# Expert scatter of a two-layer flow-matching step on one core: single passes over a high and a low part, and two units of the next job ahead of it

## The reference, cut to what matters

```
for e in range(N_EXPERTS):
    out = out + combine[:, e:e + 1] * swiglu(xt, exp_wg[e], exp_wu[e], exp_wd[e])
```

## Time and profile before

| | |
|---|---|
| median of 3 runs | 1936.82 us (1935.96 to 1938.35) |
| profiled execution, its own time | 1934.04 us |
| its span, first to last instruction | 1932.3 us |
| mean granted TensorE clock | 0.954 |
| PE, DVE, ACT busy | 91%, 66%, 51% |

### The profile page before, as it was taken

One profiled execution on the slowest core, in us unless ns is written; L12 is line 12 of the kernel. 1 busy time (PEld: TensorE's weight loads), 2 busy tenths in 40 slices (PEclk: granted clock), 3 DMA queues, 4 the chain that ended last, 5 costly groups with the idle time before them and its releaser, 6 DMA issues.

```text
span 1932.3 us, 32651 instructions
## 1 busy us (share of the span) xinstructions
PE 1767.5 (91%) x11466; PEld 1430.8 (74%) x11466; DVE 1284.7 (66%) x1889; ACT 985.6 (51%) x1356; POOL 132.3 (7%) x208
## 2 busy tenths in 40 slices
PE   4989999977979998898669999999999999999997
PEld 2757777756768884797558788887878787878785
DVE  4345666665255551322379898989888898989897
ACT  1322222221234443122248787877777777878684
POOL 0134333330000000110000000000000000000000
PEclk8889999988989998899869999999999999999999
DMA  9531111020755437433339898988989797979790
GB/s 402 211 142 41 41 41 41 3 90 17 316 228 183 152 135 290 152 135 135 155 119 370 302 366 315 369 333 344 351 326 370 295 372 298 379 303 367 307 351 22
DMA packets 61367, 442.86 MB, mean 229 GB/s; under 512 B 7008, under 2 KB 8160, under 8 KB 10080
## 3 DMA queue, kind: packets, MB, share of 16 engines
q1 hardware_dynamic: 59184, 437.81, 59.3%
q10 hardware_dynamic: 1584, 2.79, 0.4%
q0 software_dynamic: 512, 1.05, 0.2%
HBM read 438.99 MB, written 2.62 MB: 229 GB/s over the span
## 4 chain that ended last, share of the span: by engine, by line
PE 81%; DVE 8%; issue 4%; DMA 3%; ACT 2%; POOL 1%; DVEq 0%; ACTq 0%; POOLq 0%; SPq 0%
PE PS L865 33%; PE PS L894 17%; PE PS L616 4%; PE PS L953 3%; PE PS L593 3%; PE PS L1044 2%; PE PS L699 2%; PE PS L1067 2%; PE PS L573 2%; PE PS L557 2%; DMA MIX<-w_mod 2%; PE PS L958 1%; PE PS L882 1%; DVE LO L1501 1%; PE PS L679 1%
## 5 line engine op out<-in xcount | busy, mean ns | idle before, releaser
L1501 DVE TENSOR_TENSOR LO<-W,HI 128x1024 fp32r<-128x1024 f32 x662 | 781.9, 1222 | 111.7 <-ACT HI L1101 65.2
L1101 ACT ACTIVATE HI<-W 128x1024 fp32r<-128x1024 f32 x662 | 689.7, 1062 | 137.4 <-PE PS L865 77.5
L865 PE MATMUL PS<-HI,XHI 128*128 128x512 f32 x970 | 393.5, 406 | 16.4 <-ACT XHI L1300 14.1
L865 PE MATMUL PS<-HI,XLO 128*128 128x512 f32 x970 | 380.6, 392 | 0.0
L865 PE MATMUL PS<-LO,XHI 128*128 128x512 f32 x970 | 294.8, 393 | 9.1 <-DVE LO L1501 8.5
L865 PEld LDWEIGHTS PS<-HI,XHI 128*128 128x128 f32 x970 | 183.1, 189 | 55.6 <-issue 15.8
L865 PEld LDWEIGHTS PS<-LO,XHI 128*128 128x128 f32 x970 | 181.3, 188 | 55.6 <-DVE LO L1501 16.3
L865 PEld LDWEIGHTS PS<-HI,XLO 128*128 128x128 f32 x970 | 183.5, 189 | 34.9
L894 PE MATMUL PS<-HI,HHI 128*128 128x512 f32 x484 | 188.9, 390 | 1.5 <-ACT HHI L1277 1.5
L894 PE MATMUL PS<-HI,HLO 128*128 128x512 f32 x484 | 188.3, 389 | 0.0
L894 PE MATMUL PS<-LO,HHI 128*128 128x512 f32 x484 | 145.5, 389 | 0.0
(11 more groups left out here) (285 smaller groups left out, 2160.0 us busy)
## 6 DMA issues: line engine op xcount, KB each, us to landing
W<-w_exp SPq DMA_DIRECT2D x298, 1024.0 KB, 6.9
W<-w_ffn SPq DMA_DIRECT2D x33, 1024.0 KB, 4.9
W<-w_mod SPq DMA_DIRECT2D x32, 1024.0 KB, 13.0
MIX<-w_mod SPq DMA_DIRECT2D x16, 1024.0 KB, 16.8
W<-w_rkv SPq DMA_DIRECT2D x8, 1792.0 KB, 8.2
W<-w_qkv SPq DMA_DIRECT2D x8, 1536.0 KB, 7.9
W<-w_o SPq DMA_DIRECT2D x1, 4096.0 KB, 12.0
W<-w_o SPq DMA_DIRECT2D x1, 3072.0 KB, 11.1
```

The costliest lines, as they stand in the source:

```text
L865: last = mm(PS[2 * (s % 2) + g], x[:, 2 * n + k, T * g:T * g + T], w[:, 512 * k:512 * k + 512], start=(n == 0 and k == 0 and i == 0 and le ...
L1101: fn(HI[:, u % NBUF], raw_unit(phase, u), ACT.Copy).then_inc(hi_ready, 1)
L1501: tt(LO[:, u % NBUF], raw_unit(phase, u), HI[:, u % NBUF].bitcast(F32), ALU.subtract)\
```

## The change

On PE the scatter's two-pass float32 products become two single-pass float32r products each, of a high part YHI and a low part YLO of the output with SELT, the turned selection of ones and zeros. The weight of each slot is applied before that: turn_weights turns SELR instead of SELW, and gets the slot's weight as a column, the product of SELW with a column of ones (two products, one for each group of tokens); DVE copies the column to SLOTW. ACT's copy of the output multiplies with SLOTW and writes YHI; DVE then computes bank * SLOTW - YHI into YLO, one operation for each half, before its additions, and PE waits for these (`ey_low`). YHI and YLO lie in the unused half of XHI and XLO. first_unit now does units 0 and 1 of the next job ahead of the scatter, and swiglu starts at unit 2.

```diff
+        SELT = sb("SELT", TT, F32R)
...
-        SELWT = flat[1][:, D + 2 * TT:D + 3 * TT]
...
+        SLOTW = sb("SLOTW", 1)
+        YHI, YLO = XHI[:, :, SLOTS:2 * SLOTS], XLO[:, :, SLOTS:2 * SLOTS]
...
                     for n in range(4):
-                        if phase == "ffn" or s or n:
+                        if phase == "ffn" or s or n > 1:
                             gate_up(phase, base, j, s, n, groups)
...
             def turn_weights(j):
                 pe.wait_ge(sel_ready, j + 1)
                 for g in range(G):
-                    last = nc.tensor.transpose(PS[2][:, P * g:P * g + P], SELW[:, g], IDENT)
+                    nc.tensor.transpose(PS[2][:, P * g:P * g + P], SELR[:, g].bitcast(F32), IDENT)
+                for g in range(G):
+                    last = mm(PS[2][:, TT:TT + 1], SELW[:, g], ONES[:, 0:1], start=(g == 0), stop=(g == G - 1))
                 last.then_inc(selT_psum, 1)
 
             def first_unit(j):
                 pe.wait_ge(xhi_ready, j + 1)
                 pe.wait_ge(x_split, j + 1)
-                gate_up("exp", NS * j + NS, j, 0, 0, 1)
+                for n in range(2):
+                    gate_up("exp", NS * j + NS, j, 0, n, 1)
 
             def job(j):
                 swiglu("exp", NS * j + NS, j, 1, lambda: gather(j + 1))
                 turn_weights(j + 1)
                 first_unit(j + 1)
-                pe.wait_ge(ey_sbuf, j + 1)
                 for b in range(4):
+                    if b % 2 == 0:
+                        pe.wait_ge(ey_low, 2 * j + b // 2 + 1)
                     for half in range(2):
                         c = 2 * b + half
-                        last = mm(PS[(6, 7, 1, 3)[b]][:, TT * half:TT * half + TT], YNAT[:, 0, P * c:P * c + P],
-                                  SELWT, start=True, stop=True)
+                        out = PS[(6, 7, 1, 3)[b]][:, TT * half:TT * half + TT]
+                        mm(out, YHI[:, c], SELT, start=True, stop=False)
+                        last = mm(out, YLO[:, c], SELT, start=False, stop=True)
                     last.then_inc(scat_psum, 1)
...
                 for half in range(2):
-                    last = fn(YNAT[:, 0, 512 * half:512 * half + 512], PS[4 + half], ACT.Copy)
-                last.then_inc(ey_sbuf, 1)
+                    fn(YHI[:, 4 * half:4 * half + 4], PS[4 + half].rearrange("p (c d) -> p c d", c=4), ACT.Copy,
+                       scale=SLOTW).then_inc(ey_sbuf, 1)
...
                 dve.wait_ge(selT_psum, j + 1)
-                nc.vector.tensor_copy(SELWT, PS[2][:, 0:TT]).then_inc(selT_sbuf, 1)
+                nc.vector.tensor_copy(SELT, PS[2][:, 0:TT])
+                nc.vector.tensor_copy(SLOTW, PS[2][:, TT:TT + 1]).then_inc(selT_sbuf, 1)
...
                 split("exp", 2 * FFN_LOADS + 1, j)
+                for half in range(2):
+                    dve.wait_ge(ey_sbuf, 2 * j + half + 1)
+                    stt(YLO[:, 4 * half:4 * half + 4], PS[4 + half].rearrange("p (c d) -> p c d", c=4), SLOTW,
+                        YHI[:, 4 * half:4 * half + 4].bitcast(F32), ALU.mult, ALU.subtract).then_inc(ey_low, 1)
                 for b in range(4):
```

More of the change, by code:

```diff
@@ L162, in build @@
         SELR = sb("SELR", TT, F32R).rearrange("p (g s) -> p g s", g=G)
-        sb("B1HIGH", C * TT - D - TT)
+        sb("B1MID", TT)
+        SELT = sb("SELT", TT, F32R)
+        sb("B1HIGH", C * TT - D - 3 * TT)
         HT, B = HTB[:, 0], [HTB[:, 1], HTB[:, 2], sb("B2", C * TT).rearrange("p (c t) -> p c t", c=C)]
@@ L347, in build @@
         selT_psum, selT_sbuf = sem("selT_psum"), sem("selT_sbuf")
-        ey_psum, ey_sbuf, scat_psum, scat_acc = sem("ey_psum"), sem("ey_sbuf"), sem("scat_psum"), sem("scat_acc")
+        ey_psum, ey_low, ey_sbuf, scat_psum, scat_acc = sem("ey_psum"), sem("ey_low"), sem("ey_sbuf"), sem("scat_psum"), sem("scat_acc")
         y_out, moe_done = sem("y_out"), sem("moe_done")
```

## The result

The changed kernel takes 1949.9 us (median of six runs, 1944.9 to 1956.8), the kernel before 1936.4 beside it: a ratio of 1.0074, 95% interval 1.0049 to 1.0098, so about 14 us slower. The forecast was 1943.2, in a range of 1937.5 to 1956.0. Direction and range held; the size was twice the forecast's +6.4.

A forecast was written before the change was run, and what follows sets the result against it. The boundary between jobs was taken as bound by the DVE chain from the scatter's additions, not PE's work; 0.62 + 0.09 = 0.71 us later at nine boundaries gives +6.4 us, 1943.2 against 1936.8, range 1937.5 to 1956.

The forecast's parts named there:

- Step 1: In turn_weights, two products with a column of ones add four records at 0.11 us each: +0.44 us.
- Step 2: On PE, unit 1 of the next job ahead of the scatter makes the scatter start 1.37 us later.
- Step 3: At the expert output's copy, ACT's scale (0 to 0.1 us) and DVE's two operations (0.69 us each) add 0.
- the cover: Unit 1 ahead of the scatter: PE reaches its wait at 1198.36, not 1196.99, 1.2 us after DVE's second half.
- Step 4: The scatter's 16 single-pass products at 0.11 us a record take 1.76 us for 3.47; additions start 0.61 us apart.
- the single passes don't pay: Rival at the scatter: a 256-column record costs 0.23 us, so PE keeps pacing the additions; +19 us, 1955.9; chance 0.07.
- Step 5: In weights_turned on DVE, a 128x1 copy behind the existing copy adds 0.09 us.
- The clock rival: PE's longer boundary wait lowers the granted clock to half speed for 3.2 us; +6.4 to +21 us; chance 0.17.
- main forecast: The low part of unit 2 comes 0.71 us later at nine boundaries: +6.4 us, 1940 to 1948; chance 0.55.
- the signs that were named: Profile after: scatter about 3.4 us behind last down unit, idle about 3 us, period 102.8 us, granted clock still 1.00.
- PE-bound: Rival: PE's work is the bound after all, its saved 1.27 us comes off every job; -11.4 us, 1925.4; chance 0.09.
- A wash: Rival: one-column products nearly free or slack behind unit 5 shrink the boundary's delay; +0 to +3 us; chance 0.12.

The follow-up runs named there:

- e1: The changed kernel with only unit 0 of the next job ahead of the scatter, as before; ratio 0.9975 to the kernel before, 1931.4 us.
- e4: The changed kernel with DVE's next selection moved from behind the additions to ahead of them, one job sooner; ratio 1.0014 to the kernel before.
- f1: The changed kernel with unit 0 alone ahead; DVE's selection moved mid-job, turned-selection copies behind unit 3's low part; 1917.5 us, ratio 0.9916 to the kernel before.
- f3: The changed kernel, both units ahead, with DVE's selection moved mid-job and turned-selection copies behind unit 3's low part; ratio 0.9975 to the kernel before.
- e2: The kernel before, two-pass products kept, with units 0 and 1 of the next job ahead of the scatter; ratio 1.0082 to the kernel before.
- f2: The kernel before, its PE order kept, with DVE's selection moved mid-job and turned-selection copies behind unit 3's low part; ratio 0.9935 to it.

## Why the prediction was right, and where it was off

- **What bounds the boundary** was right: the DVE chain from the additions to the low part of unit 2, not PE's work. e1, e4 and f1 to f3 move its links, and the period without a fall comes out within 0.1 us of what was expected each time. In f1 DVE's chain and PE's work are within 0.2 us of each other.
- **Step 1** had four records at 0.11; they took 0.34 together, and the two units behind them 2.87 for 2 x 1.37, 0.13 more: 0.47 for 0.44. The scatter starts 3.43 us behind the last down unit, for 3.40 forecast.
- **Step 2** was right, and it is the cause of the loss: one unit is 1.37 us, and both pairs (e1 and after without a fall, f1 and f3) differ by 1.38 and 1.37.
- **Step 3** was right in its effect, zero. DVE's operation took 0.75 us instead of 0.69; ACT's copy took 0.68 with the scale for 0.60 without, inside the 0 to 0.1 allowed. The unit that I called the cover wasn't needed: in e1 PE starts the scatter 2.05 us behind the last down unit without waiting for the low part. It needs only the first half then, and DVE starts on both halves at 1197.20, 0.76 us behind that unit.
- **Step 4**: 0.12 us a record for 0.11, additions 0.60 apart for 0.61. The rival "the single passes don't pay" is out.
- **Step 5**: 0.07 for 0.09 (the copy to SLOTW in the chain above). The sum of steps was 0.71 and is 0.72. In front of job 0 it was nothing, as forecast: from the start of the transposes to the first unit it is 1.63 us in both kernels. At the last boundary it was +0.7.
- **The clock rival came true on top of the forecast**, which is why +6.4 became +13.5. The median lies above the 1940 to 1948 of the main forecast; the range held only because it took in most of this rival, and of the signs that were named, a granted clock of 1.00 failed and a period over 103.5 pointed to the clock. The prediction put 0.17 on it, against the row it had found itself: the earlier trace rows, a fall behind a wait of 2.41 us. The argument against, that small products preceded that wait and dense ones precede this, doesn't hold; e2 falls in half its jobs at 2.35 us. The wait it forecast (3.0 from end to start, 2.79 in this view) was right; the "1.4" of before is the wait of the weight load, and the same view of the matmuls has 1.00, so the wait grew by 1.8, not by 1.6. The price was right only as an upper bound: 1.6 at nine boundaries forecast for the extreme, 0.8 to 1.5 at seven found.
- **PE-bound** fell: in the changed kernel PE is busy for 1.1 us less a job (99.78 for 100.89; 1.27 forecast), and the job gets longer. That doesn't make the single passes worthless: the additions start sooner with them, which is worth 0.66 us a job with DVE's chain as it was (e1) and 0.8 with the chain cut (f1 against f2). The change lost this to the second unit ahead. **A wash** fell with the periods.
- The Trainium skill ("TensorE: Matmul & The Clock Gate", why this matters for your kernels) warns of idle gaps between bursts. The runs agree with the direction of that: no inner job has a fall up to a wait of 1.44 us, three of eight at 1.75 and seven at 2.79.

Left open: why some boundaries fall and others with the same wait don't. In e2 they alternate; nothing in these runs was varied to tell what decides it. Nor was it tried how much of the medians' spread from run to run comes from the number of falls. Part of it comes from elsewhere: the first job's end lies between 1082.8 and 1091.1 us in the ten profiled executions, which is why the periods say more than the medians.

## What to carry to other kernels

Work moved ahead of a step that starts another engine's chain is not free just because the first engine has it to do anyway: ask which wait ends last behind it, and what work is left there as cover. When a saving is to be made on an engine that is 99% busy, first look where the remaining 1% lies; here cutting what stood needlessly in DVE's chain was worth 1.26 us a job, more than the 0.66 to 0.8 that the single passes brought. A wait of TensorE that grows from 1.0 to over 1.7 us between dense stretches can cost 0.8 to 1.5 us on top of its own length, so compare the granted clock by stretch, not only the wait.

## What the runs showed of the hardware that was not expected

- The clock falls behind waits as short as 1.75 us between dense matmuls, at some boundaries and not at others (table above), and eight useless matmuls in such a wait made the kernel faster (102.78 us a job for 103.6 to 104.3).
- ACT's copy of 128x512 takes 0.684 us with a per-partition scale against 0.596 without. The Trainium skill ("ScalarE: Activation LUTs", What ACT_TABLE_LOAD costs) puts a per-partition operand at about 93 ns, and this agrees. DVE's operation of two tensors and a per-partition scalar takes 0.746 us against 0.687 for an addition of the same size.
- A product with one column is not free: four records in 0.34 us, 0.085 each, and the unit behind them took 1.49 us instead of 1.37 (e1).
- Before and after, the scatter of a job is 16 records of 256 columns: the change doesn't lower their number. A record of a float32 product took 0.217 us (3.47/16), one of a float32r product 0.12, and that alone brings the scatter from 3.47 us to 1.90.
